# A state-space stage that scans every fourth token, with its channel chunks passed through a scratch in memory

## What is computed

```python
bu_re = einsum('blgc,gpc->blgp', u, bb_re); bu_im = einsum('blgc,gpc->blgp', u, bb_im)
x = associative_scan(complex: x_t = a * x_(t-1) + bu_t)            # 64 groups of 16 channels, 64 states each
y = einsum('blgp,gcp->blgc', x_re, c_re) - einsum('blgp,gcp->blgc', x_im, c_im)
g = gelu(y + d_skip * u)
ga, gb = split(g @ w_glu); return ga * sigmoid(gb)
```

## Time and profile before

| | us |
|---|---|
| median of 3 runs (2959.12 to 2964.72) | 2961.07 |
| profiled execution | 2959.73 |
| its span, first to last instruction | 2957.9 |

### The profile page before, as it was taken

One profiled execution on the slowest core, in us unless ns is written; L12 is line 12 of the kernel. 1 busy time (PEld: TensorE's weight loads), 2 busy tenths in 40 slices (PEclk: granted clock), 3 DMA queues, 4 the chain that ended last, 5 costly groups with the idle time before them and its releaser, 6 DMA issues.

```text
span 2957.9 us, 28891 instructions
## 1 busy us (share of the span) xinstructions
PE 2792.2 (94%) x11348; PEld 1991.8 (67%) x11348; DVE 1404.8 (47%) x2231; ACT 539.1 (18%) x1019; POOL 860.2 (29%) x688
## 2 busy tenths in 40 slices
PE   8999999999999999999999899999994469999999
PEld 7888884755448888875446547888442124688888
DVE  6454312166526544232496434555317991466521
ACT  2000000111101000011121522222015430222200
POOL 5444320000324444410000323442014650344432
PEclk9999999999999999997799999999996679999999
DMA  6555321211125454221011002224210002122222
GB/s 225 169 171 167 100 96 57 71 52 48 43 86 167 164 171 160 86 72 43 27 59 57 29 29 72 93 92 124 68 52 16 0 1 86 58 92 92 83 79 68
DMA packets 222626, 253.37 MB, mean 86 GB/s; under 512 B 16328, under 2 KB 209180, under 8 KB 222364
## 3 DMA queue, kind: packets, MB, share of 16 engines
q1 hardware_dynamic: 207996, 199.32, 20.9%
q10 hardware_dynamic: 14496, 52.21, 5.1%
HBM read 249.41 MB, written 2.10 MB: 85 GB/s over the span
## 4 chain that ended last, share of the span: by engine, by line
PE 83%; DVE 12%; ACT 2%; issue 1%; POOL 1%; SPq 0%; DMA 0%; DVEq 0%; POOLq 0%
PE ps L612 36%; PE ps L668 13%; PE ps L1134 9%; PE ps L498 5%; PE ps L1600 4%; PE ps L2271 4%; DVE phase L2429 2%; PE ps L1161 1%; PE ps L1641 1%; PE ps L1653 1%; DVE phase L2414 1%; PE ps L893 1%; PE ps L1269 1%; DVE rs L1850 1%; DVE act_t L2371 1%
## 5 line engine op out<-in xcount | busy, mean ns | idle before, releaser
L612 PE MATMUL ps<-hT,ring 128*128 128x256 f32 x2816 | 653.6, 380 | 3.8 <-ACT hT L1039 1.4
L612 PEld LDWEIGHTS ps<-hT,ring 128*128 128x128 f32 x2816 | 534.2, 190 | 80.9 <-issue 4.1
L612 PE MATMUL ps<-phase,ring 128*128 128x256 f32 x2112 | 498.5, 379 | 0.4 <-DVE phase L561 0.4
L540 POOL TENSOR_TENSOR ring<-ring 128x512 f32<-128x512 f32 (+1 forms) x124 | 161.1, 1299 | 1005.8 <-DMA ring<-in_ffn_w 515.2
L612 PEld LDWEIGHTS ps<-phase,ring 128*128 128x128 f32 x2112 | 400.4, 190 | 54.7 <-issue 0.8
L668 PE MATMUL ps<-phase,ring 128*128 128x256 f32 x1848 | 400.6, 379 | 1.0 <-issue 1.0
L668 PEld LDWEIGHTS ps<-phase,ring 128*128 128x128 f32 x1848 | 350.7, 190 | 48.8 <-issue 1.4
L1134 PE MATMUL ps<-hT,ring 128*128 128x512 f32 x512 | 227.9, 599 | 3.1 <-ACT phase L1326 2.5
L1600 PE MATMUL ps<-hT,ring 128*128 128x512 f32 x448 | 198.2, 599 | 0.9 <-ACT hT L1039 0.9
L543 POOL TENSOR_TENSOR ring<-ring 128x512 f32<-128x512 f32 (+1 forms) x124 | 191.1, 1541 | 0.0
L694 DVE TENSOR_TENSOR act_t<-u,ps 128x256 f32<-128x256 f32 x176 | 73.4, 421 | 235.6 <-PE ps L612 235.3
(11 more groups left out here) (333 smaller groups left out, 3141.2 us busy)
## 6 DMA issues: line engine op xcount, KB each, us to landing
ring<-in_ffn_w SPq DMA_DIRECT2D x60, 1024.0 KB, 5.2
ring<-in_ffn_w_up SPq DMA_DIRECT2D x44, 1024.0 KB, 5.1
phase<-in_ada_w ACTq DMA_DIRECT2D x64, 512.0 KB, 3.9
ring<-in_w_in SPq DMA_DIRECT2D x19, 1024.0 KB, 5.1
sq<-in_ada_w ACTq DMA_DIRECT2D x32, 512.0 KB, 4.1
ring<-in_attn_w_in SPq DMA_DIRECT2D x14, 1024.0 KB, 5.0
ring<-in_ffn_w_down SPq DMA_DIRECT2D x8, 1408.0 KB, 6.1
ring<-in_ssm_w_glu SPq DMA_DIRECT2D x8, 1024.0 KB, 5.5
```

Source lines behind the costliest of these rows:

```text
L540: pool.tensor_tensor(s1, a21, a22, ALU.add).then_inc(combined, 1)
L612: mm = pe.matmul(ps[:, 4 * w + bank_of[name], 0:HALF], left[:, c], right[name](c), start=(opens and c == 0), stop=(c == KC // 2 - 1), skip ...
```

## The change

Four tokens make one scan step. A unit is now a whole chunk of 128 channels: four pairs of groups, 128 steps each, eight units. The norm orders tokens by their residue modulo 4. ACT sends each shifted chunk to a scratch `u_dram` from its own queue (`ssm_store`); SP brings it back stacked in eight moves (`ssm_moves`). Between the tokens of one step a direct product replaces the even and odd matrices and the skip: its matrices are made by PE after (1, 1), in part from B in a second layout (`b_own`, loaded by `ssm_own_loads`), and set in place by 32 moves (`ssm_place_direct`). GELU writes rows that go out to `y_dram` and come back into `hT` in eight moves a chunk. C is loaded later (`ssm_c_loads`) and turned at (0, 0). The parameters need 63 small steps for 32, the powers of the pole 12 operations each on DVE and POOL. `glu` takes four chunks early for six.

```diff
...
-STEPS = np.broadcast_to(np.arange(2, T + 1, 2), (P, T // 2)).astype(np.float32)
+STRIDE = 4
+NK = T // STRIDE
+STEPS = np.broadcast_to(np.arange(STRIDE, T + 1, STRIDE), (P, NK)).astype(np.float32)
...
+                if q == 2:
+                    ssm_c_loads(sp)
...
-        NK = T // 2
-        SSM_UNITS = PAIRS // 2
+        GC = 16
+        SSM_UNITS = KC
...
+            for n, name in enumerate(("ssm_b_re_2", "ssm_b_im_2")):
+                src = a[name][0].rearrange("(u g j) s c -> g j s u c", g=2, j=2)
+                for g in range(2):
+                    for j in range(2):
+                        sp.dma_start(b_in[n][g * HD:(g + 1) * HD, j:PAIRS:2, :], src[g, j]).then_inc(s_sin3, 16)
...
+        def ssm_c_loads(sp):
+            sp.wait_ge(tile_done, TILE0["ffn2"] + EVENTS[2]["tile", 0] - 1)
+            for n, name in enumerate(("ssm_c_re_2", "ssm_c_im_2")):
+                sp.dma_start(c_in[n], a[name][0].rearrange("(k g) c s -> (g c) k s", g=8)).then_inc(s_cin, 16)
+
+        def ssm_own_loads(sp):
+            sp.wait_ge(s_cz, 4)
             for n, name in enumerate(("ssm_b_re_2", "ssm_b_im_2")):
-                sp.dma_start(b_in[n], a[name][0].rearrange("(j g) s c -> (g s) j c", g=2)).then_inc(s_sin3, 16)
-            for n, name in enumerate(("ssm_c_re_2", "ssm_c_im_2")):
-                sp.dma_start(c_in[n], a[name][0].rearrange("(k g) c s -> (g c) k s", g=8)).then_inc(s_sin3, 16)
+                sp.dma_start(b_own[n], a[name][0].rearrange("(v j) s c -> (j s) v c", j=2)).then_inc(s_cin, 16)
+
+        def ssm_place_direct(sp):
+            sp.wait_ge(s_drow, 4)
+            sp.wait_ge(s_zero, 1)
+            for j in range(2):
+                for u in range(2):
+                    for g in range(2):
+                        for l in range(STRIDE):
+                            src = 32 * (2 * u + g) + GC * j
+                            to = 64 * j + GC * l
+                            sp.dma_start(direct[to:to + GC, u:2 * KC:2, g, GC * l:],
+                                         direct_rows[src:src + GC, :, 0:GC * (STRIDE - l)]).then_inc(s_dir, 16)
...
+            dve.wait_ge(s_cin, 32)
+            dve.wait_ge(gated, 3 * FC)
+            for k in range(2):
+                for g, name in enumerate(("group_even", "group_odd")):
+                    dve.tensor_scalar(cz[k][:, :, g, :], c_in[k], C(name), None, ALU.mult).then_inc(s_cz, 1)
...
+            product("A2", "A", "A")
+            product("A3", "A2", "A")
+            product("A4", "A2", "A2")
+            product("C1", "C0", "A")
+            product("C2", "C0", "A2")
+            product("C3", "C0", "A3")
+            tt("DEC", "DEC", "DEC", ALU.mult)
+            tt("DEC", "DEC", "DEC", ALU.mult)
             assert at[0] == SMALL_STEPS
...
+        def ssm_ca(eng, n, signal, other):
+
+            eng.wait_ge(signal, 1)
+            eng.wait_ge(other, 1)
+            for i in range(1, 5):
+                re, im = (par[:, r[i], :].unsqueeze(2).to_broadcast([P, PAIRS, GC]) for r in (POLE_RE, POLE_IM))
+                at = 1 + 3 * (i - 1)
+                if i > 1:
+                    eng.wait_ge(signal, at)
+                eng.tensor_tensor(CA[n][:, :, i, :], CA[n][:, :, 0, :], re, ALU.mult).then_inc(signal, 1)
+                eng.tensor_tensor(ca_part[n], CA[1 - n][:, :, 0, :], im, ALU.mult).then_inc(signal, 1)
+                eng.wait_ge(signal, at + 2)
+                eng.tensor_tensor(CA[n][:, :, i, :], CA[n][:, :, i, :], ca_part[n], ALU.add if n == 0 else ALU.subtract)\
+                    .then_inc(signal, 1)
+
+        CA_STEPS = 1 + 3 * 4
...
+            if (q, half) == (1, 1):
+                pe.wait_ge(s_bz, BZ_STEPS)
+                pe.wait_ge(s_ca, CA_STEPS)
+                pe.wait_ge(s_cap, CA_STEPS)
+                for p in range(PAIRS):
+                    rows_of = slice(32 * (p % 4), 32 * (p % 4) + 32)
+                    for n in range(2):
+                        mm = pe.matmul(ps[rows_of, 6, (p // 4) * HD:(p // 4 + 1) * HD],
+                                       b_wide[n][:, p, :, :], CA[n][:, p, 0:4, :], start=(n == 0), stop=(n == 1))
+                mm.then_inc(s_par, 1)
+            if (q, half) in ((2, 0), (2, 1)):
+                n = half
+                pe.wait_ge(s_parc, 8 + 4 * n)
+                turn(pe, bz_flat[n], 4, 2 * KC).then_inc(s_par, 1)
...
+            dve.wait_ge(s_cin, 64)
             for k in range(2):
-                for g, name in enumerate(("group_even", "group_odd")):
-                    dve.tensor_scalar(cz[k][:, :, g, :], c_in[k], C(name), None, ALU.mult).then_inc(s_bz, 1)
-
-        def ssm_ca(eng, n, signal):
-
-            eng.wait_ge(s_parc, 13)
-            re, im = (par[:, r, :].unsqueeze(2).to_broadcast([P, PAIRS, 32]) for r in (POLE_RE, POLE_IM))
-
-            def of_pairs(x):
-                return x.rearrange("p c (q s) -> p (c q) s", q=4)
-
-            eng.tensor_tensor(of_pairs(CA[n]), of_pairs(CT[n]), re, ALU.mult).then_inc(signal, 1)
-            eng.tensor_tensor(of_pairs(ca_part[n]), of_pairs(CT[1 - n]), im, ALU.mult).then_inc(signal, 1)
-            eng.wait_ge(signal, 2)
-            eng.tensor_tensor(CA[n], CA[n], ca_part[n], ALU.add if n == 0 else ALU.subtract).then_inc(signal, 1)
-
-
-        s_stack = sem("ssm_stacked")
+                dve.memset(b_wide[k], 0.0).then_inc(s_bz, 1)
+            own_re, own_im = (par[:, r, :].unsqueeze(2).to_broadcast([P, PAIRS, GC]) for r in (OWN_RE, OWN_IM))
+            n += 2
+            for k, op in enumerate((ALU.subtract, ALU.add)):
+                dve.wait_ge(s_bz, n)
+                dve.tensor_tensor(bt[0], b_own[k], own_re, ALU.mult).then_inc(s_bz, 1)
+                dve.tensor_tensor(zt, b_own[1 - k], own_im, ALU.mult).then_inc(s_bz, 1)
+                dve.wait_ge(s_bz, n + 2)
+                for j in range(2):
+                    rows_of = slice(j * HD, (j + 1) * HD)
+                    dve.tensor_tensor(b_wide[k][rows_of, :, j, :], bt[0][rows_of], zt[rows_of], op).then_inc(s_bz, 1)
+                n += 4
+            dve.wait_ge(s_bz, n)
+            ssm_ca(dve, 0, s_ca, s_cap)
...
+            dve.wait_ge(s_drow, 3)
+            dve.wait_ge(s_parc, 8)
+            dve.tensor_tensor(direct_rows[:, :, 0:GC], direct_rows[:, :, 0:GC], skip_rows, ALU.add).then_inc(s_drow, 1)
...
+                if b == 2:
+                    ssm_moves(sp)
                 load_slot(sp, n3 + 2 * b, w[:, :, b * WCOL:(b + 1) * WCOL])
                 load_slot(sp, n3 + 2 * b + 1, w[:, :, D + b * WCOL:D + (b + 1) * WCOL])
 
-        def tokens(x, odd):
-
-            return x.rearrange("p (k r) -> p r k", r=2)[:, odd, :]
-
-        GLU_EARLY = 6
+        def ssm_moves(sp):
+
+            def back(c):
+                sp.wait_ge(s_yrow[c % 2], 16 * (c // 2 + 1))
+                rows_of = y_dram[c].rearrange("(j i x) (v k) -> j v x i k", j=2, i=STRIDE, v=4)
+                for j in range(2):
+                    for v in range(4):
+                        to = 32 * v + GC * j
+                        sp.dma_start(hT[to:to + GC, c, :].rearrange("p (i k) -> p i k", i=STRIDE), rows_of[j, v])                            .then_inc(s_back[c], 16)
+
+            for c in range(KC):
+                sp.wait_ge(s_urow[c], 16)
+                if c >= 2:
+                    sp.wait_ge(s_bu, 2 * (c - 1))
+                rows_of = u_dram[c].rearrange("(v j x) (i k) -> j i x v k", j=2, v=4, i=STRIDE)
+                for j in range(2):
+                    for i in range(STRIDE):
+                        to = 64 * j + GC * i
+                        sp.dma_start(stacked[to:to + GC, c % 2, :].rearrange("p (v k) -> p v k", v=4), rows_of[j, i])                            .then_inc(s_stack[c % 2], 16)
+                if c >= 4:
+                    back(c - 4)
+            for c in range(KC - 4, KC):
+                back(c)
+
+        def ssm_store(act, c):
+            act.wait_ge(h_ready, h_before(6) + c + 1)
+            act.dma_start(u_dram[c], hT[:, c, :]).then_inc(s_urow[c], 16)
+
+        GLU_EARLY = 4
...
+            pe.wait_ge(s_zero, 3)
+            for c in range(SSM_UNITS + 2):
+                if c < SSM_UNITS:
+                    pe.wait_ge(s_stack[c % 2], 128 * (c // 2 + 1))
+                    if c >= 2:
+                        pe.wait_ge(s_pre, 4 * (c - 2) + 4)
                     for n in range(2):
-                        for j in range(2):
-                            rows_of = slice(64 * j, 64 * j + 64)
-                            mm = pe.matmul(ps[:, 2 * (u % 2) + j, n * NK:(n + 1) * NK], BT[n][rows_of, u, :],
-                                           sq[rows_of, c % 2, (u % 2) * NK:(u % 2 + 1) * NK], start=True, stop=True)
-                    mm.then_inc(s_bu, 1)
-                if u >= 2:
-                    v = u - 2
-                    c = v // 2
-                    even, odd = (ps[:, 4 + 2 * (c % 2) + k, 0:NK] for k in range(2))
-                    if v % 2 == 0:
```

(59 more changed lines are left out.)

362 lines of the change are left out of this document (184 added, 178 removed).

## The result

The changed kernel takes 2910.7 us (median of four runs, 2908.9 to 2913.7) against 2960.1 us for the kernel before on the same chip: a ratio of 0.983, 95% interval 0.981 to 0.985. It is 49 us faster; the prediction had said 2914. A second timing beside the last experiments gave 2910.8 us, ratio 0.983, interval 0.9816 to 0.9843.

The account below looks back on a forecast made before the run. VectorE was taken to bound the state-space loop, TensorE most of the rest. From 2959.7 us, 80.9 gained from the loop to the GLU product and 33.2 lost in preparation gave 2912.0; forecast 2914 us, range 2896 to 2942.

Parts of the forecast that it names:

- The loop: State-space loop: eight VectorE turns replace 16, 12.05 us each, 88.4 us from the second rotation in.
- D: In sums: last down matmul's end, 2223.5 us; as rival: stall and loop losses eat the gain, 2961 us, chance 0.03.
- D': The end of the last down matmul in the changed kernel, measured at 2254.96 us.
- I keep that mix: Loop turn: two of three VectorE rotations back stay long beside GpSimd, 1.75 and 1.66 us against 0.69.
- The start: Before the loop: chunk 0's trip through the scratch and first products, first rotation at D + 22.6.
- rival C: Loop moves: small moves serialise at 2.2 us each, a chunk's 16 take 35 us, result near 3097 us; chance 0.05.
- The tail: After the last rotation back: 11.3 us to the GLU's long run, whose product ends at D + 231.0.
- The preparation: Down stage: making the direct matrices stalls TensorE 29.0 us and moves D by +33.2 us.
- the wait for b: Down stage, after q=1: b's second-layout loads, issued behind the last down load, land at 2157.6 us; TensorE arrives at 2143.6.
- the clock: Behind the direct matrices: TensorE's granted clock needs 1.5 us (0 to 3.4) to come back after the stall.
- Rival A: Loop: something other than VectorE sets the pace, turns of 14 to 17 us, 2928 to 2949 us; chance 0.14.
- B: Down stage: the stall is short, 10 us or less, giving 2880 to 2895 us; chance 0.08.

Follow-up runs that it names:

- small-fraction run: The changed kernel with the fraction steps of units 2 to 7 on 8 columns instead of 128: 2907.4 us, ratio 0.9812.
- tail experiment: The changed kernel with the GLU product reordered so TensorE works on the second output block while the last chunk is away: 2904.0 us, ratio 0.9804.
- run without a stall: The changed kernel with b loaded earlier and the direct matrices asked for later, both together: 2881.3 us, ratio 0.9725.

## Why the prediction was right, point by point

**The loop.** Predicted: turn 12.05 us, without fractions 10.2, the 88.4 us from the second rotation, its end at D + 116.5. Measured: 12.03, 10.14, 88.1 (2282.79 to 2370.92), D' + 116.0. The sum was right, one sentence of it wrong: "I keep that mix". It holds in the turns without fractions (1.75 and 1.64 us) and fails in the others. The step that failed is the division of the time lost beside GpSimd, and the sums under the small-fraction run show why the total held all the same: a turn with fractions lost 3.0 us before and loses 2.97 now, wherever it falls. A turn costed by its undisturbed rows, 0.69 us for a rotation back and 1.14 for four fractions, would have come out 3.0 us short, and one without fractions 2.0, some 21 us over the loop. That the sum came within 0.02 us is partly luck: +2.3 in the fractions and -2.1 in the rotations back, and the prediction gave no reason why the loss should keep its size. The eight scans were 3.76 us, 0.2 more than the four, and the fractions' undisturbed part rose from 0.88 to 1.14: that is the 0.4 set aside for both together, so this term was right.

**The start.** First rotation predicted D + 22.6, measured D' + 23.3; the second D + 28 and D' + 27.8. Both numbers are better than their parts. The first shift ended at D' + 9.6 and not D + 8.3, since the norm ahead of it ran later and its scale slower; the trip from there to the input product took 8.3 us and not 9.1, and the two products 5.5 for 5.2. And the second rotation was not set by the product of chunk 1, as the prediction has it: that product ended at D' + 25.9, and the rotation followed VectorE's own first rotation and fractions without idle time (23.3 + 2.4 + 2.1 = 27.8). That 28 was hit is luck. Stores landed in 2.6 us (2.4), the moves in 1.9 (2.2), in this table of DMA issues (destination and source, queue, count, KB each, median us from issue to landing):

```profile
ssm_u_rows<-hT ACTq DMA_DIRECT2D x8, 256.0 KB, 2.6
sq<-ssm_u_rows SPq DMA_DIRECT2D x64, 32.0 KB, 1.9
hT<-ssm_y_rows SPq DMA_DIRECT2D x64, 32.0 KB, 1.8
```

The Trainium skill, DMA: Bandwidth & Descriptors (Bandwidth), which says that transfers under 64 KB are ruled by their descriptors, fits these rows as far as they go: an eighth of the bytes takes 1.9 us where 256 KB take 2.6, though those go the other way. But what it made one fear, rival C, would need this time to be paid in series, and eight moves take 3.6 us of SP's queue when nothing holds them, 0.45 each (3.7 to 5.0 us in the middle of the loop). C decides from 1.1 us a move; even sixteen halved moves took 8.68 us, 0.54 each.

**The tail.** Predicted 11.3 us from the last rotation back to the GLU's long run, measured 10.8; predicted 100.7 + 2.5 us for the 234, measured 103.46, of which 2.8 for the clock, by the tail experiment's 0.430 us each and by the windows. Product end predicted D + 231.0, measured D' + 230.2.

**The preparation.** Predicted +33.2 us, measured +31.5 with 1.6 us of it older than the stage, so +29.9. Three terms, two of them mis-sized:
- the wait for b: predicted 2157.6 - 2143.6 = 14.0 us behind TensorE's arrival, measured 2156.2 - 2145.1 = 11.1. The prediction put b's landing 7.5 us behind that of the weight load ahead. That load took 6.3 us here, from about 2145.1, so it was in at 2151.4, and b followed 4.5 us later. The chain behind it: 15.0 predicted, 15.8 measured (the two clearings 0.91 each, not 0.7). Stall 27.0 for 29.0.
- the clock: 1.5 us were set aside for coming back behind the direct matrices. The down product behind them took 19.18 us for 44, 19.05 when nothing stood ahead: 0.1 us. In this run the low clock is paid in the direct matrices themselves (3.6 us for 128 records, 2.0 in the run without a stall; predicted 3.4). The run with b loaded early paid 1.2 us more behind them, so the prediction's 0 to 3.4 was the right way to put it.
- the small steps ended at 2097.9 (2097), TensorE asked at 2105.8: hidden, as said. The 24 B products ended at 2136.8, in the range given. The 32 placements took 20.9 us of SP, 0.65 each and not 0.42; hidden all the same. The turns and the parameters' turns came as costed.

**The sum and the rivals.** 2912.0 us was said for the profiled execution, which took 2910.7 (its span 2908.9); 2914 for the median, which came to 2910.7 too. Rival A (another engine paces the loop) fell with the 12.03 us turn and the tripled direct product; B (a short stall) with the 27.0 us; C (moves serialise) with the 3.6 us for eight moves and with the halved ones; D needed A.

**What the stall is worth** is the one thing that the prediction left unsaid. It costed the stall and took it as given; the experiments show that 29.4 us of the kernel were lost to one order in SP's list and one point in TensorE's, neither of which the new scan needs.
